# Gate rows from split sums, the last chunk's weights multiplied by the gate row, and a residual buffer of its own

## What is computed

```python
mod = silu(c) @ w_ada + b_ada                       # (1, 3*2048)
shift, scale, gate = split(mod, 3)
h = rms_norm(x, norm_g) * (1 + scale) + shift
proj = h @ w_in                                     # three branches, their gates, merge gates
...
merged = (g_pool * (y_pool @ w_branch_pool) + g_attn * (y_attn @ w_branch_attn)
          + g_conv * (y_conv @ w_branch_conv))
x = x + gate[:, None] * (merged @ w_out)
return rms_norm(x, final_g)
```

## Time and profile before

| | |
|---|---|
| median of 3 runs | 947.83 us (947.66 to 948.02) |
| the profiled execution | 947.48 us, of it the span of the core 945.4 us |
| TensorE busy | 911.3 us (96%) |
| VectorE busy | 691.7 us (73%) |
| ScalarE busy | 419.6 us (44%) |
| chain that ended last | TensorE 92%, VectorE 2%, ScalarE 2%, transfers 2% |

### The profile page before, as it was taken

The page is one execution under the profiler, slowest core; times in us unless marked ns, Lnnn a source line. Parts: engine busy times, 40 slices in busy tenths (PEclk is TensorE's granted clock), DMA queues, the critical chain, the costliest instruction groups (busy, mean ns, idle before and its releaser), DMA issues.

```text
span 945.4 us, 10234 instructions
## 1 busy us (share of the span) xinstructions
PE 911.3 (96%) x4195; PEld 732.3 (77%) x4195; DVE 691.7 (73%) x780; ACT 419.6 (44%) x382; POOL 9.9 (1%) x27
## 2 busy tenths in 40 slices
PE   1899999999999999999999999999999999999996
PEld 1567677888888888888877777888888888888884
DVE  4767696878968777767778886685686978856653
ACT  3436243645344334443375655347434343434342
POOL 2000000000000000000000000000000000000000
PEclk9999999999999999999999999999999999999998
DMA  9999999955446656655545456657779999955512
GB/s 333 387 386 387 339 354 371 319 199 178 137 158 207 211 179 193 208 179 177 181 135 174 138 160 148 212 166 155 269 248 394 376 316 310 323 207 183 179 45 89
DMA packets 108494, 220.01 MB, mean 233 GB/s; under 512 B 3888, under 2 KB 4480, under 8 KB 107680
## 3 DMA queue, kind: packets, MB, share of 16 engines
q1 hardware_dynamic: 106752, 213.15, 66.6%
q0 software_dynamic: 1120, 5.43, 1.5%
q10 hardware_dynamic: 576, 0.79, 0.2%
HBM read 217.25 MB, written 2.10 MB: 232 GB/s over the span
## 4 chain that ended last, share of the span: by engine, by line
PE 92%; DVE 2%; DMA 2%; ACT 2%; SPq 1%; issue 1%; ACTq 0%; DVEq 0%
PE acc_even L1157 13%; PE acc_even L1159 13%; PE acc_even L1158 13%; PE acc_odd L1157 13%; PE acc_odd L1158 13%; PE acc_odd L1159 12%; PE side_a L1157 2%; PE side_a L1159 2%; PE side_a L1158 2%; PE side_b L1199 2%; DMA raw<-in_w_ada 2%; PE side_b L1157 1%; PE side_b L1159 1%; PE side_b L1158 1%; PE side_a L1184 1%; PE side_b L1184 1%
## 5 line engine op out<-in xcount | busy, mean ns | idle before, releaser
L709 DVE TENSOR_TENSOR wl<-raw,wh 128x2048 fp32r<-128x2048 f32 x151 | 345.3, 2290 | 165.7 <-ACT wh L446 165.3
L446 ACT ACTIVATE wh<-raw 128x2048 fp32r<-128x2048 f32 x151 | 288.1, 1913 | 282.0 <-PE acc_even L1159 109.4
L1157 PE MATMUL acc_even<-wh,act_h 128*128 128x512 f32 x432 | 172.0, 398 | 2.6 <-DVE act_l L789 2.2
L1157 PE MATMUL acc_odd<-wh,act_h 128*128 128x512 f32 x432 | 169.9, 393 | 0.2 <-DVE wl L709 0.2
L1159 PE MATMUL acc_even<-wh,act_l 128*128 128x512 f32 x432 | 169.1, 391 | 0.0
L1158 PE MATMUL acc_even<-wl,act_h 128*128 128x512 f32 x432 | 168.8, 391 | 0.0
L1158 PE MATMUL acc_odd<-wl,act_h 128*128 128x512 f32 x432 | 168.2, 389 | 0.0
L1159 PE MATMUL acc_odd<-wh,act_l 128*128 128x512 f32 x432 | 168.2, 389 | 0.0
L888 DVE SCALAR_TENSOR_TENSOR conv_slots<-conv_slots,taps 128x256 f32<-128x256 f32 x240 | 100.3, 480 | 0.2
L1157 PEld LDWEIGHTS acc_even<-wh,act_h 128*128 128x128 f32 x432 | 81.5, 189 | 22.7 <-issue 5.1
L1157 PEld LDWEIGHTS acc_odd<-wh,act_h 128*128 128x128 f32 x432 | 81.1, 188 | 19.6 <-issue 2.2
(11 more groups left out here) (275 smaller groups left out, 888.6 us busy)
## 6 DMA issues: line engine op xcount, KB each, us to landing
raw<-in_w_in SPq DMA_DIRECT2D x107, 1024.0 KB, 5.1
raw<-in_w_ada SPq DMA_DIRECT2D x48, 1024.0 KB, 8.8
raw<-in_w_out SPq DMA_DIRECT2D x16, 1024.0 KB, 5.0
raw<-in_w_branch_pool SPq DMA_DIRECT2D x8, 1024.0 KB, 5.0
raw<-in_w_branch_attn SPq DMA_DIRECT2D x16, 512.0 KB, 6.7
raw<-in_w_branch_conv SPq DMA_DIRECT2D x8, 1024.0 KB, 6.9
raw<-in_conv_pw SPq DMA_DIRECT2D x4, 1024.0 KB, 6.4
x_tok<-in_x SPq DMA_DIRECT2D x2, 1024.0 KB, 9.3
```

What stands on the lines that cost most here:

```text
L446: nc.scalar.activation(wh[:, m % RING], raw[SLOT_OF[g]][:, :, :], ACT.Copy).then_inc(high_done, 1)
L709: nc.vector.tensor_tensor(wl[:, m % RING], raw[SLOT_OF[load_of(m)]][:, :, :], wh[:, m % RING].bitcast(F32), ALU.subtract).then_inc(raw_don ...
L1157: nc.tensor.matmul(sums, xh, wh[:, slot, i, :], start=begin, stop=False)
```

## The change

1. The gate sums are split like the weights: ScalarE copies them to `gate_high` (and once ones to `ones_high`), VectorE takes the remainder as `gate_low`, which lies where the sums did, and TensorE makes two fp32r matmuls in place of one in f32.
2. The four pieces of o3 are multiplied by the gate row, in place in their raw buffer, ahead of their split: by VectorE in `gate_weights`, called from VectorE's `split`. ScalarE's high half waits for it. The residual of o3 needs no product then.
3. For o3 the residual is written to `out_tmp`, from which ScalarE squares, while VectorE writes its product with final_g to `x_res`.
4. ScalarE's share of the output is scaled and stored in one part of 768 columns.

```diff
+    gate_high = at("gate_high", [P, COLS], F32R, 201 * KB + 384)
+    gate_low = at("gate_low", [P, COLS], F32R, 201 * KB + 2944)
+    ones_high = at("ones_high", [P, P], F32R, 201 * KB + 2432)
...
@@ scalar: split
                     if m >= RING:
                         act.wait_ge(used, m - RING + 1)
+                    if m >= M_END - RING:
+                        act.wait_ge(weights_gated, m - M_END + RING + 1)
...
@@ scalar: square_result
-                nc.scalar.activation(square_dump, x_res[:, h, bass.ts(j, COLS)], ACT.Square,
+                res = out_tmp[:, h, :] if j == 3 else x_res[:, h, bass.ts(j, COLS)]
+                nc.scalar.activation(square_dump, res, ACT.Square,
...
@@ scalar: the loop
+                if m in (113, 119, 125, 131):
+                    q = (m - 113) // 6
+                    act.wait_ge(raw_done, raws(LOAD_OF["gate", q, 3]))
+                    if q:
+                        act.wait_ge(gate_rows_mm, q)
+                    else:
+                        nc.scalar.activation(ones_high[:, :], ones[:, :], ACT.Copy)
+                    nc.scalar.activation(gate_high[:, :], gate_sums[:, :], ACT.Copy).then_inc(sums_high, 1)
...
@@ scalar: the tail
-                for n, (lo, hi) in enumerate(((SHARE, SHARE + 448), (SHARE + 448, D_MODEL))):
-                    some = x_res[:, h, lo:hi]
-                    nc.scalar.activation(some, some, ACT.Copy, scale=out_rstd[:, h:h + 1]).then_inc(out_high, 1)
-                    act.wait_ge(out_high, 2 * h + n + 1)
-                    act.dma_start(out_rows[:, h, lo:hi], some).then_inc(stored, 16)
+                some = x_res[:, h, SHARE:D_MODEL]
+                nc.scalar.activation(some, some, ACT.Copy, scale=out_rstd[:, h:h + 1]).then_inc(out_high, 1)
+                act.wait_ge(out_high, h + 1)
+                act.dma_start(out_rows[:, h, SHARE:D_MODEL], some).then_inc(stored, 16)
...
@@ vector: split
+                    if m >= M_END - RING:
+                        gate_weights(m)
                     dve.wait_ge(high_done, m + 1)
...
+            def gate_weights(m):
+                g = load_of(m)
+                dve.wait_ge(loaded[SLOT_OF[g]], landed(g))
+                dve.wait_ge(gate_added, QUARTERS)
+                weights = raw[SLOT_OF[g]][:, :, :]
+                row = gate_rows[:, 3 * COLS:D_MODEL].unsqueeze(1).broadcast_to([P, PK, COLS])
+                nc.vector.tensor_tensor(weights, weights, row, ALU.mult).then_inc(weights_gated, 1)
...
@@ vector: the loop
+                if m in (113, 119, 125, 131):
+                    dve.wait_ge(sums_high, (m - 113) // 6 + 1)
+                    nc.vector.tensor_tensor(gate_low[:, :], gate_sums[:, :], gate_high[:, :].bitcast(F32), ALU.subtract
+                                            ).then_inc(sums_low, 1)
...
@@ vector: the tail
-                chained(nc.vector.tensor_tensor(out_tmp[:, h, :], sums_of("o3")[:, h, :], gate_rows[:, cols],
-                                                ALU.mult))
-                nc.vector.tensor_tensor(rest, rest, out_tmp[:, h, :], ALU.add).then_inc(res_ready, 1)
+                nc.vector.tensor_tensor(out_tmp[:, h, :], sums_of("o3")[:, h, :], rest, ALU.add).then_inc(res_ready, 1)
+                dve.wait_ge(res_ready, 4 + h)
+                nc.vector.tensor_tensor(rest, out_tmp[:, h, :], final_rows[:, cols], ALU.mult)
                 dve.wait_ge(res_squared, 3 * TH + h + 1)
...
-                chained(nc.vector.tensor_tensor(rest, rest, final_rows[:, cols], ALU.mult))
...
@@ tensor: the loop
-                    pe.wait_ge(raw_done, raws(LOAD_OF["gate", q, 3]))
+                    pe.wait_ge(sums_low, q + 1)
...
-                    nc.tensor.matmul(pa[:, 0:COLS], ones[:, :], gate_sums[:, :], start=True, stop=True
+                    nc.tensor.matmul(pa[:, 0:COLS], ones_high[:, :], gate_high[:, :], start=True, stop=False)
+                    nc.tensor.matmul(pa[:, 0:COLS], ones_high[:, :], gate_low[:, :], start=False, stop=True
                                      ).then_inc(gate_rows_mm, 1)
```

More of the change, by code:

```diff
@@ L284, in program @@
         gate_summed, gate_rows_mm, gate_added = sem("gate_summed"), sem("gate_rows_mm"), sem("gate_added")
+        sums_high, sums_low, weights_gated = sem("gate_sums_high"), sem("gate_sums_low"), sem("weights_gated")
         res_ready, res_squared = sem("res_ready"), sem("res_squared")
@@ L391, in _ @@
                     sp.dma_start(out_rows[:, h, cols], x_res[:, h, cols]).then_inc(stored, 16)
-            sp.wait_ge(stored, 16 * 4 * TH)
+            sp.wait_ge(stored, 16 * 3 * TH)
         @block.gpsimd
```

## The result

The changed kernel takes 951.35 us in the median (950.01 to 952.59, 6 runs); the kernel before, beside it, 947.91 (947.66 to 948.7, 6 runs). The ratio is 1.0035, with a 95% interval of 1.0022 to 1.0048: slower by 0.35%, clear of no change. The profiled execution took 951.37 us, of it the span 949.4, 4.0 us more than before.

A forecast was written before the change was run, and what follows sets the result against it. TensorE, busy 911.3 of 945.4 us, was taken to bound the kernel. Terms -1.1 + 4.1 + 1.4 - 1.1 = +3.3 on 947.48 give 950.8, beside the median 951.1; stated 951.0, range 948.8 to 952.8.

The forecast's parts named there:

- gap and fall of the clock: Forecast's own case: TensorE idles in o3 and its clock then falls; 951.0 us, own range 949.9 to 952.5, chance 0.62.
- Part 1: Gate matmuls: split sums save 1.6 us, waits in quarters 0 and 2 give back some 0.5; net -1.1 us.
- Part 2, the gap: In o3, multiplying weights ahead of their split makes piece 151 late, its low half ending at 926.34; TensorE gap +4.1 us.
- The serial line: In o3, multiplication, high half and low half run one behind the other, piece after piece; 6.48 us per piece.
- to refill the array: TensorE's restart behind the o3 gap, counted in the gap at 0.1 us or so.
- The clock: TensorE's granted clock falls to half in or just behind the o3 gap; +1.4 us.
- Part 3: Tail behind the last matmul: one step of 0.73 less, reciprocal 0.37 earlier, merged transfer 0; together -1.1 us.
- B: Rival: multiplications fall into VectorE's idle time, piece 151 ready before 922.5, no gap; -2.2, 945.3 to 945.6 us, chance 0.08.
- A: Rival: the o3 gap without the fall of the clock; +1.9, 949.4 to 949.7 us, chance 0.22.
- C: Rival: half the o3 gap, 1.5 to 2.5 us, and the clock holds; 947 to 948.2 us, chance 0.08.

The follow-up runs named there:

- e3: The kernel before with only the gate rows from split sums added; 946.74 us, ratio 0.9987.
- e2: The changed kernel with 16 unused matmuls on TensorE ahead of its wait for piece 151 in the first token half; 950.36 us, ratio 1.0023.
- e8: The changed kernel with 8 unused matmuls on TensorE ahead of its wait for piece 151; 949.97 us, ratio 1.002.
- e6: The changed kernel with o3's multiplications one piece ahead and ScalarE's output share again in two parts, a transfer for each; 945.98 us, ratio 0.9975.
- e1: The changed kernel with VectorE multiplying o3's piece m + 1 ahead of the low half of piece m; 945.51 us, ratio 0.9974.

## Why the prediction was right

The forecast was 951.0, the time is 951.35, and the case was the one taken: gap and fall of the clock. The terms are off by one to four tenths each, and part of that cancels: the gap came out larger, part 1 brought less, the tail gave more. The profiled execution also carries the 0.46 of its start, which no term had.

- **Part 1** (-1.1): -0.95 in the trace, -1.1 in e3. The waits came in quarters 0 and 2, as worked out; with the first matmul behind each wait (0.50 in place of 0.39, which the sum left out here) they gave back 0.65 us in place of 0.5. ones_high took 0.31 us, the copy 0.62 to 0.63, the subtraction 0.69.
- **Part 2, the gap** (+4.1, ready at 926.34): the low half ended at 926.12 in a run that stood 0.53 earlier at that place, so 0.3 later than worked out. The serial line took 6.56 us per piece, not 6.48: the multiplication's end to the high half's start, and the high half's end to the low half's, are a few hundredths longer each, which over four pieces makes the 0.3. TensorE waited 0.40 for piece 150 and 3.50 for piece 151 by the timeline. The gap as a whole is 4.5 us, the 5.85 less the clock's 1.3, where the sum has 4.1. The sum's 0.1 "to refill the array" is seen only as a longer first matmul behind a wait, 0.50 in place of 0.39; no run shows the cause. The gap began at 922.5, not near 921.5: o3 began 0.6 later than a saving of 1.1 would have it, mostly from the start, and piece 150 held TensorE up for longer than worked out.
- **The clock** (+1.4): gap and clock together are 5.85 in the trace where I had 5.5; e2 and e8 put the clock's part at 1.3 by their traces, e8 at 1.4 by its median. The fall came about 0.5 us before the restart (0.93 in the mean over 3.5 us is 0.5 at half), so most of the slow stretch, some 2.9 us, fell on work.
- **Part 3** (-1.1): -1.3. The sum's step came as worked out: from the last matmul's end to the square it is 0.72 us less. The reciprocal gave 0.30, not 0.37: it begins 0.1 behind the root's end, where I had 0.03. I had set the merged transfer at 0; the remaining 0.3 stands behind the reciprocal, and by e6 the transfer gives as much. Here the Trainium skill says (Trainium Kernel Development and Optimization, Key Constraints) that transfers issued from several engines run on the same 16 DMA engines, and that issuing from more of them saves only the issuing time. That agrees with the full DMA share in that most of the merging gives nothing; the rest may come from the packets (288 on ScalarE's queue in place of 576; over two full microseconds 395 GB/s flow from 946 on in the change, 379 from 942 on before) or from the last issue, 0.8 us earlier in e1 than in e6; no run tells these apart.
- **The rivals.** B decides by when piece 151 is ready. In e1, where the multiplications are moved so that it is ready in time, the kernel takes 945.51, the time given for B (945.3 to 945.6). A is e8, where a little filling holds the clock: 949.97, given as 949.4 to 949.7; it is 0.3 above that, with a gap 0.4 larger than worked out. C, half the gap with the clock held, did not come: the waits are 0.40 and 3.50. The Trainium skill's rule (TensorE: Matmul & The Clock Gate, What's actually happening) that the moment of switching isn't tied to the kernel's start agrees with the start of the program, which is the same in all versions: the clock was low from about 38.4 us for 3.4 us in the profile before, from about 34.7 for 6.8 in that of the change, and not at all from 20 to 50 us in e2. The six runs of the change reach from 950.01 to 952.59, more widely than the six before (947.66 to 948.7). Whether some of them had no fall in the gap isn't shown, since only one execution has a profile.
- **The chances.** Added up as the prediction says, the forecast and the rivals give slower 0.69, same 0.23, faster 0.08, not the 0.71, 0.19 and 0.10 that it states.

What stays open: which gaps the clock bears in this place. It held through 1.73 us behind 1.8 us of filling and fell in the 3.50; nothing between was run.

## What to carry to other kernels

Work added on an engine with idle time is free only if it can enter that idle time. Where two engines hand a piece to and fro, look at the order of the program: a step placed behind the last step of the piece before makes a serial line of what was a pipeline, and the same step one piece earlier fills the waits. And price a gap of TensorE with what comes behind it, not by its length alone.

## What the runs showed of the hardware

A matmul of 128x512 in f32 held TensorE for 0.86 us, one in fp32r for 0.23 (0.227 in a long row). TensorE's restart after a wait costs little while the clock is up: the first matmul takes 0.50 in place of 0.39. After 3.5 us without work it took 0.79, and the five behind it 0.43 each in the chain in place of 0.23. Not expected was how the start of the program varies. The clock was low for 3.4 us near 38 us in the profile before, for 6.8 us in that of the change and in e3, and not at all in e2. But that didn't set the time: e2, which had no fall there, came to the first matmul into side_b behind 99.5 us at 100.18, later than the change (100.04) and the kernel before (99.58). The change's execution was already 0.41 of its 0.46 us behind at the step on shift_rows (34.15 against 33.74), with the clock still at its upper level, after longer waits for w_ada. Such a scatter of the start is part of what a change of this size is measured against.
